# The gate columns in full fp32 inside the first key product, two weight blocks split ahead of the normalisation, and two weight sums in one operation

## What is computed

```python
h = rmsnorm(x, g1)                       # x: 544 rows of 1024
z = h @ w_in                             # key, query, value columns of the mLSTM, ... and 8 gate columns
ig = z[mi] + b_if[0]; lf = log_sigmoid(z[mf] + b_if[1])   # 4 heads each
```

## Time and profile before

| | |
|---|---|
| median of 3 runs | 1013.2 us (1012.11 to 1013.21) |
| profiled execution | 1012.78 us, of which the span is 1011.0 |
| TensorE busy | 980.3 us (97%) |
| VectorE busy | 684.7 us (68%) |
| ScalarE busy | 464.0 us (46%) |
| GpSimd busy | 161.3 us (16%) |

### The profile page before, as it was taken

The page is one execution under the profiler, slowest core; times in us unless marked ns, Lnnn a source line. Parts: engine busy times, 40 slices in busy tenths (PEclk is TensorE's granted clock), DMA queues, the critical chain, the costliest instruction groups (busy, mean ns, idle before and its releaser), DMA issues.

```text
span 1011.0 us, 20145 instructions
## 1 busy us (share of the span) xinstructions
PE 980.3 (97%) x7816; PEld 959.4 (95%) x7816; DVE 684.7 (68%) x1170; ACT 464.0 (46%) x966; POOL 161.3 (16%) x341
## 2 busy tenths in 40 slices
PE   5999999999999999999999999999999999999996
PEld 4999999998999998999999999999999999999996
DVE  6877656578665898777775547777777777634341
ACT  5665545467554656555554434333344333322221
POOL 2000112120020312111012211211211111111010
PEclk9999999999999999999999999999999999999998
DMA  6523152355223232323335212222223222332302
GB/s 194 193 68 100 47 112 88 85 158 168 86 84 84 64 85 63 106 63 87 103 97 176 94 59 84 85 85 84 90 97 97 94 84 80 121 98 73 91 26 88
DMA packets 98069, 96.98 MB, mean 96 GB/s; under 512 B 4740, under 2 KB 93721, under 8 KB 97719
## 3 DMA queue, kind: packets, MB, share of 16 engines
q1 hardware_dynamic: 92879, 82.49, 27.8%
q10 hardware_dynamic: 3976, 10.36, 2.9%
q0 software_dynamic: 1120, 2.86, 0.8%
HBM read 88.38 MB, written 7.31 MB: 95 GB/s over the span
## 4 chain that ended last, share of the span: by engine, by line
PE 82%; DVE 7%; ACT 4%; issue 4%; DMA 1%; POOL 1%; ACTq 0%; DVEq 0%; POOLq 0%; SPq 0%
PE D L1626 43%; PE D L1658 28%; PE D L1643 3%; DVE w_l L1252 2%; ACT w_h L969 1%; PE X L1847 1%; PE X L1885 1%; DMA x_t<-in_x_prompt 1%; DVE acc L1592 1%; DVE ups L1582 1%; PE X L1779 1%; PE D L1743 1%; PE X L1793 1%; DVE f_x L1331 0%; PE X L1794 0%
## 5 line engine op out<-in xcount | busy, mean ns | idle before, releaser
L1252 DVE TENSOR_TENSOR w_l<-raw,w_h 128x512 fp32r<-128x512 f32 (+1 forms) x274 | 193.6, 725 | 117.6 <-ACT w_h L969 116.1
L1658 PE MATMUL D<-a_h,w_h 128*128 128x272 f32 x840 | 251.8, 300 | 3.4 <-ACT mqT L1085 1.5
L1658 PE MATMUL D<-a_h,w_l 128*128 128x272 f32 x840 | 244.4, 291 | 0.0
L1658 PE MATMUL D<-a_l,w_h 128*128 128x272 f32 x840 | 243.2, 290 | 0.0
L969 ACT ACTIVATE w_h<-raw 128x512 fp32r<-128x512 f32 (+1 forms) x274 | 164.0, 618 | 102.2 <-PE D L1626 75.7
L1658 PEld LDWEIGHTS D<-a_h,w_h 128*128 128x128 f32 x840 | 159.8, 190 | 6.1 <-ACT mqT L1085 1.7
L1658 PEld LDWEIGHTS D<-a_l,w_h 128*128 128x128 f32 x840 | 160.1, 191 | 0.0
L1658 PEld LDWEIGHTS D<-a_h,w_l 128*128 128x128 f32 x840 | 159.5, 190 | 0.0
L1626 PE MATMUL D<-h_h,w_h 128*128 128x272 f32 x704 | 145.9, 288 | 0.0
L1626 PE MATMUL D<-h_h,w_l 128*128 128x272 f32 x704 | 145.7, 288 | 0.0
L1626 PE MATMUL D<-h_l,w_h 128*128 128x272 f32 x704 | 145.1, 288 | 0.0
(11 more groups left out here) (331 smaller groups left out, 1701.8 us busy)
## 6 DMA issues: line engine op xcount, KB each, us to landing
raw<-in_w_in SPq DMA_DIRECT2D x64, 512.0 KB, 3.8
raw<-in_w_up SPq DMA_DIRECT2D x44, 512.0 KB, 4.3
raw<-in_w_down SPq DMA_DIRECT2D x16, 512.0 KB, 3.8
raw<-in_w_branch SPq DMA_DIRECT2D x12, 512.0 KB, 3.5
raw<-in_w_out SPq DMA_DIRECT2D x8, 512.0 KB, 4.5
raw<-in_w_down SPq DMA_DIRECT2D x8, 384.0 KB, 3.3
x_spill<-xT ACTq DMA_DIRECT2D x1, 2176.0 KB, 8.0
xT<-x_spill ACTq DMA_DIRECT2D x1, 2176.0 KB, 10.5
```

What stands on the lines that cost most here:

```text
L1252: v.tensor_tensor(split_view(w_l, g), whole_view(g), split_view(w_h, g).bitcast(F32), ALU.subtract)\
L1658: last = t.matmul(out, wt[:, k, :], x[:, left, k, :], start=w in (1, 2, 5) and k == i == 0, stop=k == KQ - 1 and i == 2, skip_group_check= ...
```

## The change

- The gates are no longer a split unit. Their 8 columns are copied in fp32 into an own tile `gate_w` of 36 columns (heads at 0 and 32), zeroed by GpSimd first. On TensorE the product is done inside the first key product (`gates_and_wait`): at each block k, two full fp32 matmuls of `gate_w[:, k]` with the two halves of `f_x[:, k]`, and then the six of the key product. They wait for `f_ready`, the key matmuls for `al_ready` as the gates did.
- The first key block's units are now 0 and 1, and both engines split them ahead of the normalisation; units 2 and 3 after it.
- VectorE's step `left` 1, which overwrites part of `f_x`, waits for the gate product.
- The nine small loads are issued by ScalarE behind x_sample, no longer by SP.
- For the pairs whose two items lie in neighbouring slots (`both`), w = 5 and w = 7 are one operation of 1024 elements per partition, at the place of w = 7.

```diff
@@ -290,8 +290,6 @@
 
         if kind == "p":
             return [(a[0], a[1], KQ, 0)]
-        if kind == "if":
-            return [(("if", 0), 0, KD, 0)]
         if kind == "mk":
             return [((("mk", a[0] // 2), half), 0, KQ, P * (a[0] % 2)) for half in range(2)]
...
@@ -314,7 +312,7 @@
             if kind == "p":
                 items = [(a[0], k) for k in range(2)]
             else:
-                items = [u[0]] if kind != "if" else []
+                items = [u[0]]
             for it in items:
                 if it not in ITEMS:
                     ITEMS.append(it)
...
 
+
+    both = [q for q in pairs if ITEMS.index((q, 0)) % NRAW + 1 == ITEMS.index((q, 1)) % NRAW]
     for q in pairs:
         u6 = u_of(q, 6) - AHEAD
-        for w, e in ((7, u6 - 3), (6, u6 - 2), (5, u_of(q, 5) - AHEAD - 2), (4, u_of(q, 4) - AHEAD - 2)):
+        for w, e in ((7, u6 - 3), (6, u6 - 2), (5, u6 - 3 if q in both else u_of(q, 5) - AHEAD - 2),
+                     (4, u_of(q, 4) - AHEAD - 2)):
             T_MAKES.setdefault(e, []).append((q, w))
...
+        gate_w = at(44192, "gate_w", [P, KD, 36])
...
         def wait_whole(eng, g):
 
             what, w = UNITS[g][0:2]
-            if g == 0:
-                eng.wait_ge(S["if_in"], 16)
-            elif what not in pair_no:
+            if what not in pair_no:
                 wait_item(eng, what)
             elif w in QUARTER:
                 wait_item(eng, (what, QUARTER[w][0]))
...
         def _(sp):
             for c in range(4):
                 sp.dma_start(x_t[:, c, :], x_prompt[0, P * c:P * c + P, :]).then_inc(x_in[c], 16)
-            def small(dst, src):
-                sp.dma_start(dst, src).then_inc(S["small_in"], 16)
-
-            blocks = lambda ap: ap.rearrange("(j f) -> j f", f=P)
             sp.dma_start(raw_if[:], w_in[0][:, GATES_AT:GATES_AT + 2 * H].rearrange("(k p) f -> p k f", p=P))\
                 .then_inc(S["if_in"], 16)
-            small(small_a[0:8, :], blocks(norm1[0]))
-            small(small_a[8:16, :], blocks(norm2[0]))
-            small(small_a[16:28, :], w_sc_conv[0].rearrange("t (j f) -> (t j) f", f=P))
-            small(small_a[28:36, :], state_conv[0, 0].rearrange("t (j f) -> (t j) f", f=P))
-            small(small_a[36:40, :], ml_norm[0])
-            small(small_a[40:41, :], da_norm)
-            small(small_b[0:2 * JU, :], state_ffn[0, 0].rearrange("t (j f) -> (t j) f", f=P))
-            fc = w_fconv[0].rearrange("t (j f) -> (t j) f", f=P)
-            small(small_c[0:66, 0, :], fc[0:66, :])
-            small(small_c[0:66, 1, :], fc[66:132, :])
             for i, item in enumerate(ITEMS):
                 if i >= NRAW:
...
-            gates_h, gates_l = split_view(w_h, 0), split_view(w_l, 0)
-            g.memset(gates_h[:, :, H:32].bitcast(F32), 0.0)
-            g.memset(gates_l[:, :, H:32].bitcast(F32), 0.0).then_inc(S["gates_zeroed"], 1)
+            g.memset(gate_w[:], 0.0).then_inc(S["gates_zeroed"], 1)
 
             for kind, a, n in ORDER:
...
             act.dma_start(x_s[0:TS, :], x_sample[0]).then_inc(S["xs_in"], 16)
+            def small(dst, src):
+                act.dma_start(dst, src).then_inc(S["small_in"], 16)
+
+            blocks = lambda ap: ap.rearrange("(j f) -> j f", f=P)
+            small(small_a[0:8, :], blocks(norm1[0]))
...
+            small(small_c[0:66, 1, :], fc[66:132, :])
             act.wait_ge(S["const_ready"], 7)
             sc.activation(kap[:], m_half[:], ACT.Square)
...
-                if g == 0:
-                    act.wait_ge(S["gates_zeroed"], 1)
-                    for at_col, col in ((0, 0), (32, H)):
-                        last = sc.activation(split_view(w_h, 0)[:, :, at_col:at_col + H], raw_if[:, :, col:col + H],
-                                             ACT.Copy)
-                    last.then_inc(S["wh_ready"], 1)
-                else:
-                    sc.activation(split_view(w_h, g), whole_view(g), ACT.Copy).then_inc(S["wh_ready"], 1)
+                sc.activation(split_view(w_h, g), whole_view(g), ACT.Copy).then_inc(S["wh_ready"], 1)
...
+            act.wait_ge(S["gates_zeroed"], 1)
+            act.wait_ge(S["if_in"], 16)
+            for at_col, col in ((0, 0), (32, H)):
+                last = sc.activation(gate_w[:, :, at_col:at_col + H], raw_if[:, :, col:col + H], ACT.Copy)
+            last.then_inc(S["gates_ready"], 1)
             split(0)
+            split(1)
...
-                    for g in range(1, AHEAD):
+                    for g in range(2, AHEAD):
                         split(g)
...
-                if g == 0:
-                    dve.wait_ge(S["gates_zeroed"], 1)
-                    for at_col, col in ((0, 0), (32, H)):
...
+                v.tensor_tensor(split_view(w_l, g), whole_view(g), split_view(w_h, g).bitcast(F32), ALU.subtract)\
+                    .then_inc(S["wl_ready"], 1)
...
@@ -1264,7 +1253,16 @@
                     dve.wait_ge(S["wl_ready"], u_of(pairs[i - 1], w) + 1)
                 if w in (6, 4):
                     dve.wait_ge(S["t_ready"], t_no[(q, {6: 7, 4: 6}[w])] + 1)
-                v.tensor_tensor(t_view(q, w), x, y, op).then_inc(S["t_ready"], 1)
+                if q in both and w == 7:
+                    if i:
+                        dve.wait_ge(S["wl_ready"], u_of(pairs[i - 1], 5) + 1)
+                    s0 = ITEMS.index((q, 0)) % NRAW
+                    b = raw[:, s0:s0 + 2, :].rearrange("p s (k f) -> p s k f", k=KQ)
+                    v.tensor_tensor(tw[:, 0:3:2, :].rearrange("p s (k f) -> p s k f", k=KQ), b[:, :, :, P:2 * P],
+                                    raw[:, s0, :].rearrange("p (k s f) -> p s k f", k=KQ, s=2), ALU.subtract)\
+                        .then_inc(S["t_ready"], 2)
+                elif not (q in both and w == 5):
+                    v.tensor_tensor(t_view(q, w), x, y, op).then_inc(S["t_ready"], 1)
...
                     split(0)
+                    split(1)
                     wait_drained(dve, block_of[("rstd",)])
 
...
-                    for g in range(1, AHEAD):
+                    for g in range(2, AHEAD):
                         split(g)
...
@@ -1347,6 +1346,7 @@
                     elif a[0] == 1:
                         dve.wait_ge(S["s_ready"], 3)
                         dve.wait_ge(S["al_ready"], KD)
+                        dve.wait_ge(S["dense_done"], block_of[("if",)] + 1)
                         sum_left(F11, F12, a_f[:, S2], ALU.subtract)
...
+            def gates_and_wait(k):
+
+                n = block_of[("if",)]
+                if k == 0:
+                    pe.wait_ge(S["gates_ready"], 1)
+                pe.wait_ge(S["f_ready"], k + 1)
+                for half in range(2):
+                    last = t.matmul(banks(n)[0:36, half, 0:HALF], gate_w[:, k, :],
+                                    f_x[:, k, HALF * half:HALF * half + HALF], start=k == 0, stop=k == KD - 1)
+                if k == KD - 1:
+                    last.then_inc(S["dense_done"], 1)
+                pe.wait_ge(S["al_ready"], k + 1)
+
...
-                elif kind == "if":
-                    plain_product(n, lambda k: pe.wait_ge(S["al_ready"], k + 1))
                 elif kind == "mk":
-                    plain_product(n)
+                    plain_product(n, gates_and_wait if a[0] == 0 else None)
```

More of the change, by code:

```diff
@@ L545, in streaming_encoder_step @@
         for nm in (
-                "small_in late_in xs_in if_in ck_in cv_in norm_f_in x_out x_back const_ready gates_zeroed "
+                "small_in late_in xs_in if_in ck_in cv_in norm_f_in x_out x_back const_ready gates_zeroed gates_ready "
                 "dense_done act_drained dve_drained "
@@ L669, in split_view @@
         def split_view(w, g):
-            m, f = UNITS[g][2], P if g else 36
-            return w[:, g % NSPLIT, 0:m * f].rearrange("p (k f) -> p k f", k=m)
+            m = UNITS[g][2]
+            return w[:, g % NSPLIT, 0:m * P].rearrange("p (k f) -> p k f", k=m)
         def wait_item(eng, item):
@@ L939, in _ @@
             act.dma_start(x_s[0:TS, :], x_sample[0]).then_inc(S["xs_in"], 16)
+            def small(dst, src):
+                act.dma_start(dst, src).then_inc(S["small_in"], 16)
+            blocks = lambda ap: ap.rearrange("(j f) -> j f", f=P)
+            small(small_a[0:8, :], blocks(norm1[0]))
+            small(small_a[8:16, :], blocks(norm2[0]))
+            small(small_a[16:28, :], w_sc_conv[0].rearrange("t (j f) -> (t j) f", f=P))
+            small(small_a[28:36, :], state_conv[0, 0].rearrange("t (j f) -> (t j) f", f=P))
+            small(small_a[36:40, :], ml_norm[0])
+            small(small_a[40:41, :], da_norm)
+            small(small_b[0:2 * JU, :], state_ffn[0, 0].rearrange("t (j f) -> (t j) f", f=P))
+            fc = w_fconv[0].rearrange("t (j f) -> (t j) f", f=P)
+            small(small_c[0:66, 0, :], fc[0:66, :])
+            small(small_c[0:66, 1, :], fc[66:132, :])
             act.wait_ge(S["const_ready"], 7)
@@ L1243, in split @@
```

(12 more changed lines are left out.)

## The result

The kernel after takes 1017.83 us (median of 6 runs, 1015.58 to 1019.02), the kernel before 1012.91 in the same session (6 runs, 1012.11 to 1013.21). The ratio is 1.0047, 95% interval [1.0037, 1.0057]: slower by 4.9 us, above the range of 1010.3 to 1016.3. The execution with the profile took 1019.02, span 1017.2, the longest of the six, so part of its 6.2 us over the span of before is scatter.

What follows compares the result with a forecast made beforehand. VectorE was taken to set the pace up to 25 us, TensorE after it. Terms -0.6 + 0.9 - 0.2 = +0.1 us gave 1012.9 on the profiled execution, forecast 1013.3 against the runs' median 1013.2, range 1010.3 to 1016.3.

Steps and rivals of the forecast that it cites:

- The small loads: At the start, nine issues on ScalarE's queue make the fourth square of x 0.3 us late.
- The splits ahead: At the start, two weight splits ahead of the normalisation make f_x begin 1.28 us late.
- edits 1 and 2: Small loads on ScalarE's queue and splits ahead of the normalisation: f_x 1.6 us late together.
- The gates' product: In the first key product, each k takes 1.68 us; done at 32.1 against 32.75, a gain of 0.6.
- The clock in step 3: At TensorE's start, 1.2 GHz loses 1.4 us, which was hidden under VectorE and no longer is.
- The drain wait: Before the second key product, TensorE stands still 0.9 us for ScalarE's drain of the gates; start at 33.0.
- The sums: Merged sums, felt only in convolution and attention steps: value -0.2 us, bounds -1.5 and +1.5.
- rival D: Longer sum ahead of softmax steps (+0.5 at three or four places) and a second slow clock stretch: 1015.5; 6%.
- A: Gate product's fp32 at the low price, or the array shared: -3.1 us, 1010; 8%.
- B: At the start, each of nine issues on ScalarE's queue costs about 0.95 us: 1018; 12%.
- C: No slow clock at the start (-1.4), or w = 5 sum off the convolution chain (-0.6 each): 1011.0 or less; 12%.
- The likeliest case: Whole kernel: no difference that can be measured, within 2 us of 1013.2; 62%.

Runs made afterwards that it cites:

- e2: Kernel before with only the nine small loads moved to ScalarE's queue; 1012.64 us, ratio 1.0003.
- e4: Kernel after with the gate matmuls of two blocks put together, four alternations instead of eight; ratio 1.0040.
- e9: Kernel before with the gate product inside the first key product as three fp32r products, own banks, splits ahead of the normalisation; 1012.37 us, ratio 0.9993.
- e6: Kernel after with twelve filler matmuls ahead of the first gate matmul; 1014.82 us, ratio 1.0019.
- e1: Kernel before with only the merged weight sums; 1013.91 us, ratio 1.0012.
- e13: Kernel before with only one sum merged, that of the second FFN gate's second column pair; 1013.34 us, ratio 1.0009.
- e3: Kernel before with only the gate edit and the splits ahead, without the small loads and the sums; 1015.29 us, ratio 1.0021.
- e5: Kernel after with the gates written to banks 4 and 5, which the second key product doesn't need; ratio 1.0039.
- e8: Kernel after with the gates as one reduced product of the high parts, low products left out; 1011.42 us, ratio 0.9980.
- e10: Kernel before with the gates as three fp32r products inside the first key product, splits ahead, plus twelve filler matmuls; 1008.5 us, ratio 0.9956.
- e7: Kernel before with twelve filler matmuls ahead of its first gate matmul; ratio 0.9995.

## Why the prediction was wrong, by its steps

**1. The small loads.** I took 0.3 for the fourth square; it was 0.38 (10.17 against 9.79). Alone they cost nothing (e2), beside the splits about 0.7.

**2. The splits ahead: right in sum, partly by luck.** The first normalised block was to begin at 16.15 to 16.45 by the terms of edits 1 and 2; it begins at 16.13. But the 1.28 for the splits was too much and the 0.3 for the loads too little: the runs show about 0.6 and 0.7.

**3. The gates' product: the step that failed.** "Each k is 2 fp32 and 6 ordinary matmuls: 0.92 + 0.755 = 1.68 us." It is 1.99. The price of an fp32 matmul, taken at the high end, was right (0.46 against 0.457 in e4). Left out was the change between the two forms in a stream that alternates: 0.32 a block, 2.5 us over eight. The rows, from which I priced fp32, are runs of fp32 matmuls with nothing between them. The waits of the kernel before show one thing that I didn't follow up. Weight loads of those same score matmuls, 28 to 330 us, idled at issue nine times:

```profile
PEld X L1832 <- issue: 2.6, 9, 0.3
```

TensorE's busy time covered it. Whether it is the same cost isn't shown. What in the array or its weight path takes the 0.32 stays open too. The Trainium skill (TensorE: Matmul & The Clock Gate, "Weight-path perf modes") says that fast weight load is on only with 128 weights and input that isn't fp32. No run here shows whether that has a part in it; the gate weights of e9 have 36 columns and are fp32r, and show no such cost.

**The clock in step 3: right in kind, too small for the profiled execution.** "The same start at 1.2 GHz loses 1.4 us." With blocks of 1.99 and a first gate matmul at 17.05, eight blocks at full clock would end at 33.0; they end near 35.7. The clock lost 2.7 here, and e6 gets 2.5 back. It stayed at 1.2 GHz up to 23.4 us and not to about 20. I took its length from before, where TensorE did other work. But the length isn't fixed by the kernel: TensorE does the same work there in e1, e2 and e13 as in before, and their granted clock over the first 33 us is 0.90, against 0.95 in before, while e3, with the gates of after, has 0.95. So 3.4 us at 1.2 GHz was possible after the change too, and the longer stretch is in part chance.

**4. The drain wait: right.** 0.9 was predicted; TensorE shows 0.62 idle, and e5, without it, comes 0.78 sooner.

The terms add up: the second key product was predicted at 33.0 and came at 36.50. Of the 3.5, 2.5 are the alternations, 1.3 the clock, -0.25 the earlier first gate matmul (17.05 for 17.3), and -0.1 the wait.

**5. The sums: wrong sign.** "Value -0.2." e1 has +1.2 to +1.4, within the bounds of 1.5 that I named but at their far end. The mechanism is that of rival D: a 1.21 us operation ahead of a softmax maximum. I gave it +0.5 a place and three or four places. It was two places, at 0.54 each. There the sum of w = 5 came forward to a point at which VectorE was late, and the 0.07 saved by merging is too small to matter.

**The rest.** In the profiled execution 1.2 us more went between 424 us and the end, where a stretch of 1.2 GHz lies near 604 us. e1, e4, e5 and e9 have one near 600 as well; before and the nine other runs have none. It comes without the merged sums (e9) and stays away with them (e6, e8). Its cause is open.

**The rivals.** A needed fp32 at half the price: excluded by e4. B needed ScalarE's issues to take 0.95 each; they took (5.02 - 1.19)/9 = 0.43, and e2 is neutral. C went the other way in both halves: the start kept its slow stretch, and the sums lost time. D's 1015.5 had the mechanism of the sums and a second slow stretch, but nothing of the alternations. The likeliest case failed because its gain of 0.6 in the first key product rested on a pitch that no row of the trace had shown.

## What to carry to other kernels

Price a change of precision inside a stream of matmuls by its alternations as well as by its matmuls: here 0.32 us for each return trip, on top of 0.91 for two fp32 matmuls in place of 0.75 for six reduced ones. In this kernel the small product was worth moving into the large one only in the large one's own form, as in e9. Where TensorE's slow stretch lay under another engine's work it cost nothing; ask of each change that makes TensorE the bound there whether it exposes that stretch, and price the fillers by the distance (-2.5 us in after, -1.4 from e9 to e10, 0 in before), not by the whole time (-2.8, -3.9, 0), in which slow stretches elsewhere come and go. Look for the place of a lengthened operation where its engine is late, whatever pair or stage it belongs to, and for every such place, not for the first that explains the wait.

## What the runs showed of the hardware

- Alternating full fp32 and fp32r matmuls costs 0.32 us a round, of which the record shows 0.12 in the fp32 pair and 0.10 in the fp32r pair on either side. By this price eight alternations cost 2.5 us and four (e4) half of that. Three fp32r products in the same place (e9) cost nothing of the kind.
- A full fp32 matmul of 128 rows, 36 columns of weights and 272 moving columns takes 0.457 us (after and e4 together).
- Twelve matmuls of 512 columns ahead of the work, in a gap of 3 us, kept the granted clock at 1.00 from 14 to 30 us in e6, e7 and e10.
- TensorE's stretch at 1.2 GHz at the start is about 3.4 us long in some executions and 6.8 in others, with the same start (granted clock over the first 33 us 0.95 in before, 0.90 in e1). Over all of e3 the granted clock is 0.991 in the five executions of 1012.87 to 1013.82 us and 0.987 to 0.990 in the six of 1015.29 to 1016.56.
- Nine small loads issued on ScalarE took 3.83 us, 0.28 to 0.66 each. Alone that costs nothing (e2, ratio 1.0003); beside the splits the first normalised block begins about 0.7 later.
